# One block in place of two: the prologue of a two-layer transformer kernel is merged into its first projections

## The chip, the cores and the metric

The program runs on one core of a Trainium2 chip. Its time is the time of one execution on the device, in microseconds (us); lower is better. The core has five engines with a queue of instructions each: TensorE (PE in the rows, its weight loads PEld), VectorE (DVE), ScalarE (ACT), GpSimd (POOL) and SyncE (SP), which here only starts transfers. Queues run in order, and engines wait for each other through semaphores.

## The reference, cut to what matters

```python
D_MODEL, SEQ, CTX_LEN = 1024, 1024, 256
mod = jax.nn.silu(c) @ ada_w[l] + ada_b[l]            # 6 x 1024 values, of c and of c_ctx
sh1, sc1, g1, sh2, sc2, g2 = split(mod, 6)
hc = modulate(rms_norm(ctx, norm1_g[l]), csh1, csc1)  # 256 tokens
hx = modulate(rms_norm(x, norm1_g[l]), sh1, sc1)      # 1024 tokens
cb, cc, cx, r, k, v, w_lo, a_lo, g_lo = split_proj(h @ lp["w_in"])
...                                                   # scan, output, feed-forward, second layer
def rms_norm(x, g): return x * rsqrt(mean(x * x, -1) + eps) * g
def modulate(h, shift, scale): return h * (1 + scale) + shift
```

The change touches only this beginning: the modulation of the first norm, the norm itself, and the order of the first products with `w_in`. The scan, the feed-forward part and the second layer stay as they are.

## The kernel before, in words

The 1280 tokens (256 of the context, 1024 of the sequence) stand in columns, the 1024 features in 8 tiles of 128 partitions. They are worked in three column groups g: 0 is the context (256 columns), 1 and 2 are the halves of the sequence (512 columns each). All data is float32.

`prologue` is a block of its own. TensorE forms the modulation for shift and scale in 8 groups of weights (`ada`, 1 MB each, three slots): 16 matmuls of 128x128 weights with the two columns of `silu_c`, in `L173`. Between them, after groups 1, 3 and 5, it adds the squares of a column group over the features: 8 matmuls with a matrix of ones (`sums`, L165). ScalarE makes the squares (L188) and the square root (L193); VectorE the reciprocal and the product with the inputs (L206, L208), then, when the modulation is there, `full` (L227): 8 instructions that scale and shift one feature tile each. A high half `h_hi` is rounded from it by ScalarE in one copy of a column group (L197), and the low half `h_lo` is the difference, three feature tiles of it by GpSimd (L243) and five by VectorE (L236). At the end of the block all engines meet and the semaphores are cleared.

`projections` is the next block. A product (`dense`) of one weight tile with one column group is a chunk: 8 feature tiles times 3 matmuls (high by high, high by low, low by high), 24 matmuls in L106. Chunks rotate over 4 PSUM banks. A weight tile is loaded to `raw_in` by SP (L336), rounded by ScalarE (`hi`, L543) and its low half taken by GpSimd (`lo`, L701); one `raw_in` serves all tiles, so the next load waits for `lo`. The first five chunks are `w` of the groups 0, 1, 2 and then `g` of 1, 2; then come `v`, `k`, `r`, and `cc`, `v` of pair 1, `cx` and so on.

Beside them runs the rest of the modulation, 32 rows of `ada_rows` (512 KB each, four slots). ScalarE's queue starts their loads between its other work (`load_mod`, L607), and VectorE multiplies and adds each (`modulation`, L756, L759). VectorE's queue has 18 of them ahead of the keys of group 0, 4 more ahead of the keys of group 1, 4 ahead of group 2, 6 behind, and then `normed`, `products_rk` and `biases`, for which ScalarE's `tanhs` waits, and behind that ScalarE's `hi` of `cx` and GpSimd's `lo` of it.

Of the kernel before, what the change touches and what calls it, by code (L numbers as in the profile page):

```python
# [21 lines left out]
P = 128  # L22
D = 1024
# [88 lines left out]
def prologue(nc, d, t):  # L112


    groups = [(0, CTX, 1), (CTX, BANK, 0), (CTX + BANK, BANK, 0)]
# [4 lines left out]
    with ExitStack() as st:  # L120
        sem = Sems(nc, st, "a_")
        sb = lambda n, s, dt=F32: st.enter_context(nc.sbuf_tensor("a_" + n, s, dt))
        xin = sb("xin", [P, KD, TOK])
        tmp = sb("tmp", [P, KD, TOK])
        rstd = sb("rstd", [P, TOK])
        adaw = sb("adaw", [P, SLOTS_ADA, NADA, KD, P])
        silu_c = t["silu_c"]
        gain = sb("gain", [P, 2, KD])
        ps = [st.enter_context(nc.psum_tensor(f"a_ps{n}", [P, BANK], F32)) for n in range(4)]
        modps = ps[3][:, 0:32].rearrange("p (n c) -> p n c", c=2)  # L130
        vec, con = t["vec"], t["con"]
        block = st.enter_context(nc.Block())

        @block.sync
        def _(sp):
            sp.dma_start(vec, d["vecs"]).then_inc(sem("vecs"), 16)
            sp.dma_start(con, d["consts"]).then_inc(sem("consts"), 16)
            sp.dma_start(xin[:, :, 0:CTX], d["ctxT"]).then_inc(sem("x0"), 16)

            sp.dma_start(t["c_row"], d["c_in"].broadcast_to([P, D])).then_inc(sem("c_row"), 16)  # L140

            def load_ada(i):
                if i >= SLOTS_ADA:
# [12 lines left out]
        @block.tensor
        def _(pe):
            pe.wait_ge(sem("consts"), 16)
            pe.wait_ge(sem("silu_c"), 1)

            def sums(g):
                at, n, _ = groups[g]
                pe.wait_ge(sem("squares"), g + 1)
# [2777 lines left out]
```

## Time and profile before

| | us |
|---|---|
| median of 3 runs | 2723.29 |
| lowest, highest | 2720.49, 2728.4 |
| the profiled execution, its own time | 2734.07 |
| its span (first to last instruction) | 2732.3 |

Busy shares of the span: TensorE 85%, VectorE 53%, ScalarE 30%, GpSimd 21%. The profile gives the granted clock of TensorE as a mean of 0.917 of full speed. A share over the whole span tells little about the first 210 us, which the change touches; the rows below are of this stretch.

### The profile page before, as it was taken

How to read it: one execution, taken by the hardware profiler on the slowest of the kernel's cores; microseconds unless marked ns; L12 is line 12 of the kernel's file. 1: busy time of each engine (PE TensorE's matmuls, PEld its weight loads, DVE VectorE, ACT ScalarE, POOL GpSimd, SP SyncE). 2: the span in 40 equal slices, each digit the busy share in tenths (PEclk: the TensorE clock that was granted, in tenths of full speed). 3: DMA queues.
4: the chain of work that ended last, by engine and by line, in shares of the span. 5: the costliest groups of instructions: out<-in, count | busy, mean ns of one | idle time of the engine just before them, and what ended most of it. 6: DMA issues, size and time to landing. Idle time of an engine off the chain costs nothing. (4 is left out here: it accounts for less than half of the span.)

```text
span 2732.3 us, 45148 instructions
## 1 busy us (share of the span) xinstructions
PE 2311.8 (85%) x18624; PEld 1864.0 (68%) x18624; DVE 1459.6 (53%) x1855; ACT 812.5 (30%) x1228; POOL 575.7 (21%) x241
## 2 busy tenths in 40 slices
PE   8598987935899969679999996888949999999898
PEld 6476665634889937568788885667738767766566
DVE  1575675748767353446666665111073566644653
ACT  2223333311333331423333332222233344423321
POOL 0313333310000023122222221324232211111111
PEclk8699999976999979889999998999969999999999
DMA  6172342365666451011222223333121111111411
GB/s 233 72 249 74 94 137 73 95 193 128 157 156 153 110 220 47 16 39 69 73 73 74 75 74 119 134 121 129 36 73 59 70 45 49 47 55 39 170 69 70
DMA packets 258244, 271.09 MB, mean 99 GB/s; under 512 B 173080, under 2 KB 208536, under 8 KB 250784
## 3 DMA queue, kind: packets, MB, share of 16 engines
q1 hardware_dynamic: 253472, 251.94, 28.6%
q10 hardware_dynamic: 4608, 16.78, 1.7%
q8 instruction: 126, 2.06, 0.3%
q14 instruction: 38, 0.31, 0.0%
HBM read 200.48 MB, written 68.19 MB: 98 GB/s over the span
## 5 line engine op out<-in xcount | busy, mean ns | idle before, releaser
L106 PE MATMUL e_ps<-h_hi,e_w_hi 128*128 128x512 f32 x704 | 276.1, 392 | 33.1 <-POOL e_w_lo L1942 33.1
L1966 DVE SCALAR_TENSOR_TENSOR e_acc<-e_grid,vec,e_acc 128x1024 f32<-128x1024 f32 x176 | 264.3, 1502 | 42.8 <-DVE e_acc L1966 37.4
L106 PE MATMUL e_ps<-h_hi,e_w_lo 128*128 128x512 f32 x704 | 274.8, 390 | 0.0
L106 PE MATMUL e_ps<-h_lo,e_w_hi 128*128 128x512 f32 x704 | 274.8, 390 | 0.0
L106 PE MATMUL b_ps<-h_hi,b_w_hi 128*128 128x512 f32 (+1 forms) x488 | 196.0, 402 | 72.2 <-POOL b_w_lo L701 42.9
L1942 POOL TENSOR_TENSOR e_w_lo<-raw_up,e_w_hi 128x1024 fp32r<-128x1024 f32 x44 | 116.2, 2642 | 372.2 <-ACT e_w_hi L1913 372.2
L106 PE MATMUL g_ps<-h_hi,g_w_hi 128*128 128x512 f32 x392 | 160.6, 410 | 40.1 <-POOL g_w_lo L2580 35.2
L2580 POOL TENSOR_TENSOR g_w_lo<-raw,g_w_hi 128x1024 fp32r<-128x1024 f32 x38 | 92.9, 2445 | 472.9 <-ACT g_w_hi L2451 472.9
L106 PE MATMUL b_ps<-h_lo,b_w_hi 128*128 128x512 f32 (+1 forms) x488 | 189.5, 388 | 0.0
L106 PE MATMUL b_ps<-h_hi,b_w_lo 128*128 128x512 f32 (+1 forms) x488 | 189.4, 388 | 0.0
L2070 PE MATMUL f_ps<-f_z_hi,f_w_hi 128*128 128x512 f32 x352 | 141.3, 401 | 49.6 <-DVE f_z_lo L2118 39.8
L106 PEld LDWEIGHTS e_ps<-h_hi,e_w_hi 128*128 128x128 f32 x704 | 132.7, 188 | 66.1 <-issue 38.9
L106 PEld LDWEIGHTS b_ps<-h_hi,b_w_hi 128*128 128x128 f32 x488 | 97.9, 201 | 106.2 <-issue 46.2
L106 PE MATMUL g_ps<-h_lo,g_w_hi 128*128 128x512 f32 x392 | 154.8, 395 | 0.0
L106 PE MATMUL g_ps<-h_hi,g_w_lo 128*128 128x512 f32 x392 | 154.5, 394 | 0.0
L106 PEld LDWEIGHTS e_ps<-h_hi,e_w_lo 128*128 128x128 f32 x704 | 132.6, 188 | 27.9
L106 PEld LDWEIGHTS e_ps<-h_lo,e_w_hi 128*128 128x128 f32 x704 | 132.8, 189 | 26.9
L2070 PE MATMUL f_ps<-f_z_lo,f_w_hi 128*128 128x512 f32 x352 | 139.6, 397 | 0.0
L2070 PE MATMUL f_ps<-f_z_hi,f_w_lo 128*128 128x512 f32 x352 | 139.5, 396 | 0.0
L2024 POOL TENSOR_TENSOR f_w_lo<-raw_down,f_w_hi 128x2816 fp32r<-128x2816 f32 x15 | 93.6, 6242 | 196.3 <-ACT f_w_hi L2052 196.3
L2108 DVE SCALAR_TENSOR_TENSOR x<-f_ps,mod,x 128x512 f32 (+1 forms) x16 | 12.0, 751 | 203.4 <-PE f_ps L2070 203.4
L2070 PEld LDWEIGHTS f_ps<-f_z_hi,f_w_hi 128*128 128x128 f32 x352 | 67.7, 192 | 68.5 <-issue 35.8
(338 smaller groups left out, 5147.0 us busy)
## 6 DMA issues: line engine op xcount, KB each, us to landing
raw_up<-w_ffn SPq DMA_DIRECT2D x22, 1024.0 KB, 5.0
raw_down<-w_down SPq DMA_DIRECT2D x16, 1408.0 KB, 6.1
c_op<-ops SPq DMA_DIRECT2D x40, 512.0 KB, 4.4
raw<-w SPq DMA_DIRECT2D x38, 512.0 KB, 3.5
b_ops<-ada_rows ACTq DMA_DIRECT2D x32, 512.0 KB, 5.2
ops<-b_ops SPq DMA_DIRECT2D x16, 1024.0 KB, 4.9
raw_in<-w SPq DMA_DIRECT2D x26, 512.0 KB, 4.6
zs<-e_z SPq DMA_DIRECT2D x22, 512.0 KB, 2.6
```

The lines of the kernel that those rows point to most:

```text
L106: last = nc.tensor.matmul(out, w[:, k, :], x[:, k, cols], start=(k == 0 and n == 0), stop=(k == nk - 1 and n == 2))
L1942: nc.gpsimd.tensor_tensor(w_lo[:, s], raw[:, s], w_hi[:, s].bitcast(F32), ALU.subtract).then_inc(sem(f"lo{s}"), 1)
L1966: a = nc.vector.scalar_tensor_tensor(out=acc[:], in0=view, scalar=wt, in1=acc[:], op0=ALU.mult, op1=ALU.add)
L2024: nc.gpsimd.tensor_tensor(w_lo[:, s], raw[:, s], w_hi[:, s].bitcast(F32), ALU.subtract).then_inc(sem(f"lo{s}"), 1)
L2070: mm = nc.tensor.matmul(ps[s][:], w[:, s, k], y[:, k], start=(k == 0 and n == 0), stop=(k == NFF - 1 and n == 2))
L2108: nc.vector.scalar_tensor_tensor(out=xs, in0=ps[s][:].unsqueeze(1), scalar=t["mod"][:, 0, bass.ds(held(nc.vector, tile + 40), 1)], in1=xs, ...
L2580: nc.gpsimd.tensor_tensor(w_lo[:, w % 2], raw[:, w % 2], w_hi[:, w % 2].bitcast(F32), ALU.subtract).then_inc(sem("lo"), 1)
```

## The change

Both functions become one block, `projections`. In it:

- the loads are issued in another order: first group of `ada` second, the constants behind the context;
- VectorE adds the 8 tiles of squares up to 2 in two instructions (`folded`), and TensorE's `sums` has 2 matmuls in place of 8;
- `h_hi` is written by ScalarE straight from the normed inputs, feature tile by feature tile, with gain and shift in the instruction (`inputs_hi`, 8 instructions for a column group). `full` remains on VectorE and feeds only `h_lo`. The low half of group 0 is VectorE's alone;
- the end of the prologue's block with its clearing of semaphores is gone;
- the first chunks are `w` 0, `w` 1, `g` 1, `w` 2, `g` 2, and each `w` waits for its own column group only;
- the slots of the 32 row loads, and the later tensors, share memory with the inputs, so the first row load waits for the last low half; 16, 20 and 24 rows stand ahead of the keys of the three groups where 18, 22 and 26 stood.

```diff
-def prologue(nc, d, t):
...
-                for k in range(KD):
-                    mm = nc.tensor.matmul(ps[g][:, 0:n], t["c_ones"], tmp[:, k, at:at + n],
-                                          start=(k == 0), stop=(k == KD - 1))
...
+            def sums(g):
+                pe.wait_ge(sem("folded"), 2 * g + 2)
+                for kt in range(2):
+                    mm = nc.tensor.matmul(ps[g][:, 0:width(g)], t["c_ones"], tmp[:, kt, cols(g)], start=kt == 0, stop=kt == 1)
...
             def dense(x, n, g):
+                if n == 0 and x == "w":
+                    pe.wait_ge(sem("h_lo"), g + 1)
+                    if g:
+                        pe.wait_ge(sem("h_lo_pool"), g)
...
             def load_mod(i):
-                if i >= MOD_SLOTS:
+                if i < MOD_SLOTS:
+                    act.wait_ge(sem("h_lo"), 3)
+                    act.wait_ge(sem("h_lo_pool"), 2)
...
+            def inputs_hi(g):
+                act.wait_ge(sem("gain"), 1)
+                act.wait_ge(sem("normed"), g + 1)
+                for kt in range(KD):
+                    a = A(h_hi[:, kt, cols(g)], tmp[:, kt, cols(g)], ACT.Identity, scale=gain[:, c, kt:kt + 1],
+                          bias=t["mod"][:, c, kt:kt + 1])
...
+            hi("w", 0); inputs_hi(0); hi("g", 0); inputs_hi(1); inputs_hi(2); hi("v", 0)
...
+            lo("w", 0); lo("g", 0); inputs_lo(1); inputs_lo(2)              # GpSimd
...
+            full(0); inputs_lo(0); full(1); inputs_lo(1); full(2); inputs_lo(2)   # VectorE
...
-            for g, i in ((0, 18), (1, 22), (2, 26)):
+            for g, i in ((0, 16), (1, 20), (2, 24)):
```

TensorE's queue at the start of the program. Before (`a_adaw` is the slot of a group of `ada`, `con` the matrix of ones):

```order
L173 MATMUL a_ps<-silu_c,a_adaw 128x2 [waits a_ada0,a_silu_c,a_consts]
L173 MATMUL a_ps<-silu_c,a_adaw 128x2 x15
L173 MATMUL a_ps<-silu_c,a_adaw 128x2 [waits a_ada1]
L173 MATMUL a_ps<-silu_c,a_adaw 128x2 x15
L165 MATMUL a_ps<-a_tmp,con 128x256 [waits a_squares]
L165 MATMUL a_ps<-a_tmp,con 128x256 x7
```

And of the change (`b_ada_in` is the slot now, `b_folded` the semaphore of VectorE's folding):

```order
L315 MATMUL b_ps<-silu_c,b_ada_in 128x2 [waits b_ada_in0,b_silu_c]
L315 MATMUL b_ps<-silu_c,b_ada_in 128x2 x15
L315 MATMUL b_ps<-silu_c,b_ada_in 128x2 [waits b_ada_in1]
L315 MATMUL b_ps<-silu_c,b_ada_in 128x2 x15
L306 MATMUL b_ps<-b_tmp,con 128x256 [waits b_folded,b_consts]
L306 MATMUL b_ps<-b_tmp,con 128x256
```

Six matmuls of each `sums` are gone, the first matmul waits for the constants no more, and the first `sums` waits for VectorE.

VectorE's queue from the modulation on. Before:

```order
L218 SCALAR_TENSOR_TENSOR a_gain<-mod,vec 128x8
L227 TENSOR_SCALAR a_tmp<-a_tmp,a_gain,mod 128x256 [waits a_normed,a_gain]
L227 TENSOR_SCALAR a_tmp<-a_tmp,a_gain,mod 128x256 x7
L227 TENSOR_SCALAR a_tmp<-a_tmp,a_gain,mod 128x512 x8
L236 TENSOR_TENSOR h_lo<-a_tmp,h_hi 128x5x256 [waits a_hi]
L227 TENSOR_SCALAR a_tmp<-a_tmp,a_gain,mod 128x512 x8
L236 TENSOR_TENSOR h_lo<-a_tmp,h_hi 128x5x512 [waits a_hi] x2
```

And of the change:

```order
L832 SCALAR_TENSOR_TENSOR b_gain<-mod,vec 128x8
L840 TENSOR_SCALAR b_xin<-b_tmp,b_gain,mod 128x256 [waits b_normed,b_gain]
L840 TENSOR_SCALAR b_xin<-b_tmp,b_gain,mod 128x256 x7
L847 TENSOR_TENSOR h_lo<-b_xin,h_hi 128x8x256 [waits b_full,b_h_hi]
L840 TENSOR_SCALAR b_xin<-b_tmp,b_gain,mod 128x512 x8
L847 TENSOR_TENSOR h_lo<-b_xin,h_hi 128x5x512 [waits b_full,b_h_hi]
L840 TENSOR_SCALAR b_xin<-b_tmp,b_gain,mod 128x512 x8
L847 TENSOR_TENSOR h_lo<-b_xin,h_hi 128x5x512 [waits b_full,b_h_hi]
```

The low half of group 0 now stands directly behind `full` of group 0 and covers all eight feature tiles.

ScalarE's queue around the first products, of the change (`b_wpool` holds the rounded weights, `b_chunk` counts finished chunks, `b_xin` is the memory of the row slots; L561 and L562 read `w`, L564 reads `g`):

```order
L461 ACTIVATE b_wpool<-raw_in 128x1024 [waits b_ada_used2,b_raw]
L536 ACTIVATE h_hi<-b_tmp,mod,b_gain 128x256 [waits b_normed,b_gain]
L536 ACTIVATE h_hi<-b_tmp,mod,b_gain 128x256 x7
L461 ACTIVATE b_wpool<-raw_in 128x1024 [waits b_ada_used0,b_raw]
L536 ACTIVATE h_hi<-b_tmp,mod,b_gain 128x512 [waits b_normed,b_gain]
L536 ACTIVATE h_hi<-b_tmp,mod,b_gain 128x512 x7
...
L562 ACTIVATE b_tmp<-b_ps 64x512
L528 DMA b_xin<-ada_rows 128x1024 [waits b_h_lo_pool,b_h_lo] x4
```

The first weight tile is rounded ahead of the inputs, and the first four row loads, which stood at the head of the second block, now stand behind the reading of `w` of group 1 and wait for the last low halves.

## Rows read from the trace of the kernel before

**Rows 1.** Timeline of TensorE, 0 to 120 us: start, us, engine, line, operation, count.
```profile
13.38 13.79 PE L173 MATMUL a_ps<-silu_c,a_adaw 128*128 128x2 f32 x64 [13.38 <-DMA a_adaw<-ada]
27.03 6.28 PE L165 MATMUL a_ps<-a_tmp,con 128*128 128x256 f32 x16
33.14 11.35 PE L173 MATMUL a_ps<-silu_c,a_adaw 128*128 128x2 f32 x64
44.35 9.58 PE L165 MATMUL a_ps<-a_tmp,con 128*128 128x512 f32 x16
53.76 11.48 PE L173 MATMUL a_ps<-silu_c,a_adaw 128*128 128x2 f32 x64
65.10 9.44 PE L165 MATMUL a_ps<-a_tmp,con 128*128 128x512 f32 x16
74.38 11.59 PE L173 MATMUL a_ps<-silu_c,a_adaw 128*128 128x2 f32 x64
```
**Rows 2.** Timeline of TensorE's weight loads in the second `sums`.
```profile
47.05 0.34 PEld L165 LDWEIGHTS a_ps<-a_tmp,con 128*128 128x128 f32 x1 [0.52 <-issue]
47.90 0.34 PEld L165 LDWEIGHTS a_ps<-a_tmp,con 128*128 128x128 f32 x1 [0.52 <-issue]
```
**Rows 3.** Windows of TensorE: busy (records), granted clock, DMA share, GB/s.
```profile
32.40:36.00 3.60, 3.60 (x30) 0.95 0.01 5
36.00:44.00 8.00, 8.00 (x39) 0.50 0.38 131
119.20:124.20 5.00, 4.93 (x23) 0.50 0.59 226
160.80:164.80 4.00, 3.93 (x11) 0.50 0.77 238
```
**Rows 4.** Timeline of ScalarE, inputs as they arrive, and the transfer of one group of `ada` (issues: count, KB each, us to landing).
```profile
10.67 1.06 ACT L185 ACTIVATE c_row<-c_row 128x1024 f32<-128x1024 f32 x1 [7.17 <-DMA c_row<-c_in]
28.43 3.62 ACT L188 ACTIVATE a_tmp<-a_xin 128x4096 f32<-128x4096 f32 x1 [4.00 <-DMA a_xin<-xT]
...
a_adaw<-ada SPq DMA_DIRECT2D x8, 1024.0 KB, 8.1
```
**Rows 5.** Timelines of VectorE and GpSimd, from the modulation to the products.
```profile
86.01 0.26 DVE L213 TENSOR_TENSOR mod<-a_ps,vec 128x16 f32<-128x16 f32 x2 [2.90 <-PE a_ps L173]
94.22 8.39 DVE L227 TENSOR_SCALAR a_tmp<-a_tmp,a_gain,mod 128x512 f32<-128x512 f32 x8
106.29 2.82 DVE L236 TENSOR_TENSOR h_lo<-a_tmp,h_hi 128x2560 fp32r<-128x2560 f32 x1 [0.95 <-ACT h_hi L197]
...
96.63 3.42 POOL L243 TENSOR_TENSOR h_lo<-a_tmp,h_hi 128x1536 fp32r<-128x1536 f32 x1 [0.66 <-ACT h_hi L197]
106.34 6.05 POOL L243 TENSOR_TENSOR h_lo<-a_tmp,h_hi 128x1536 fp32r<-128x1536 f32 x1 [6.29 <-ACT h_hi L197]
116.88 2.34 POOL L701 TENSOR_TENSOR b_w_lo<-raw_in,b_w_hi 128x1024 fp32r<-128x1024 f32 x1 [4.48 <-ACT b_w_hi L543]
```
**Rows 6.** Timeline of ScalarE's row loads and the first product's start.
```profile
113.58 2.12 ACTq L607 DMA_DIRECT2D b_ops<-ada_rows  x4
...
119.27 0.58 PE L106 MATMUL b_ps<-h_hi,b_w_hi 128*128 128x256 f32 x1 [33.30 <-POOL b_w_lo L701]
```
**Rows 7.** Timeline of TensorE and VectorE, 130 to 210 us, the places where they resume.
```profile
160.87 0.69 PE L451 MATMUL b_ps<-con,b_v 128*128 128x128 f32 x2 [6.10 <-ACT b_v L562]
208.75 0.50 PE L106 MATMUL b_ps<-h_hi,b_w_hi 128*128 128x512 f32 x1 [2.34 <-POOL b_w_lo L701]
...
172.65 0.35 DVE L808 TENSOR_SCALAR b_kk<-b_k,vec 128x256 f32<-128x256 f32 x1 [9.38 <-ACT b_k L562]
202.75 0.16 DVE L764 TENSOR_SCALAR b_bias<-vec 128x4 f32<-128x4 f32 x1
```
**Rows 8.** Waits up to 230 us: total, times, longest.
```profile
ACT b_w_hi L543 <- DMA raw_in<-w: 20.2, 3, 9.3
```
**Rows 9.** Groups of VectorE, 172.5 to 203 us: count, busy, mean ns, idle before.
```profile
L756 DVE CUSTOM_DVE_ANT_0 b_ops<-b_ops,c_row 128x1024 f32<-128x1024 f32 x14 | 19.3, 1377 | 0.2 <-DMA b_ops<-ada_rows 0.2
```

More of the change, by code:

```diff
@@ L420, in dense @@
                         pe.wait_ge(sem("read_d"), dve_read[old])
[L421 removed]
+                product(nc, ps[i % 4][:, 0:width(g)], *weights(s), h_hi, h_lo, KD, cols(g)).then_inc(sem("chunk"), 1)
             def low_rank(m, j):
@@ new lines, in _ @@
+            act.wait_ge(sem("vecs"), 16)
+            A(silu_c, t["v_cc"].rearrange("p (k c) -> p k c", c=2), ACT.Silu).then_inc(sem("silu_c"), 1)
+            act.wait_ge(sem("c_in"), 16)
+            A(c_row, c_row, ACT.Silu).then_inc(sem("c_row"), 1)
+            for g in range(3):
+                act.wait_ge(sem(f"x{g}"), 16)
+                A(tmp[:, :, cols(g)], xin[:, :, cols(g)], ACT.Square).then_inc(sem("squares"), 1)
+            act.wait_ge(sem("eps"), 2)
+            for g in range(3):
+                act.wait_ge(sem("sumsq"), g + 1)
+                A(rstd[:, cols(g)], ps[g][:, 0:width(g)], ACT.Sqrt, scale=1.0 / D, bias=t["c_eps"]).then_inc(sem("std"), 1)
@@ L611, in _ @@
             hi("w", 0)
+            inputs_hi(0)
             hi("g", 0)
[L613 to L623 removed]
@@ new lines, in gains @@
+            def gains():
+                for s in range(SLOTS_ADA):
+                    dve.wait_ge(sem(f"ada_used{s}"), (GADA - 1 - s) // SLOTS_ADA + 1)
+                for c in range(2):
+                    TT(t["mod"][:, c, 0:16], modps[:, :, c], t["v_ada_b"][:, 0:16], ALU.add).then_inc(sem("mod"), 1)
+                dve.wait_ge(sem("mod"), 2)
+                for c in range(2):
+                    a = STT(out=gain[:, c], in0=t["mod"][:, c, 8:16], scalar=1.0, in1=t["v_norm1_g"], op0=ALU.add, op1=ALU.mult)
+                a.then_inc(sem("gain"), 1)
+                dve.wait_ge(sem("gain"), 1)
+                dve.wait_ge(sem("normed"), 3)
@@ new lines, in full, with inputs_lo @@
+            def full(g):
+                c = 1 if g == 0 else 0
+                for kt in range(KD):
+                    a = TS(xin[:, kt, cols(g)], tmp[:, kt, cols(g)], gain[:, c, kt:kt + 1], t["mod"][:, c, kt:kt + 1], ALU.mult, ALU.add)
+                a.then_inc(sem("full"), 1)
+            def inputs_lo(g):
+                k0 = KPOOL if g else 0
+                dve.wait_ge(sem("h_hi"), g + 1)
+                dve.wait_ge(sem("full"), g + 1)
+                TT(h_lo[:, k0:KD, cols(g)], xin[:, k0:KD, cols(g)], h_hi[:, k0:KD, cols(g)].bitcast(F32),
+                   ALU.subtract).then_inc(sem("h_lo"), 1)
@@ L859, in _ @@
+            nc.vector.memset(t["c_eps"], RMS_EPS).then_inc(sem("eps"), 1)
+            nc.vector.memset(t["c_gneps"], GN_EPS).then_inc(sem("eps"), 1)
+            folded(0)
+            inputs_normed(0)
+            folded(1)
+            folded(2)
+            inputs_normed(1)
+            inputs_normed(2)
+            gains()
+            full(0)
+            inputs_lo(0)
+            full(1)
+            inputs_lo(1)
+            full(2)
+            inputs_lo(2)
             TS(ka1[:], k_a, -1.0, 1.0, ALU.mult, ALU.add).then_inc(sem("ka1"), 1)
+            dve.wait_ge(sem("h_hi"), 3)
```

273 lines of the change are left out of this document (112 added, 161 removed).

## The prediction

> **What bounds the kernel now.** The change touches only what lies ahead of about 210 us, so I read three views of that stretch: TensorE's timeline, to see where it works and where it stands; the windows, for its clock; and the timelines of VectorE, ScalarE and GpSimd where TensorE stands.
>
> Up to 86 us TensorE is the bound. It starts at 13.38 and runs without a pause to 85.97 [rows 1], and VectorE waits for its last record [rows 5]. From start to start the four stretches of modulation take 13.65, 11.21, 11.34 and 11.59 us (47.8 for 256 records, two for each matmul) and the three `sums` 6.11, 9.41 and 9.28 us (24.8). The pace of the modulation is 8.00 us for 39 records at granted clock 0.50 (1.2 GHz) and 3.60 us for 30 at 0.95 [rows 3]. The first stretch, 13.65 us for 64 records or 0.213 each, runs at the slow pace. The later stretches save 2.1 to 2.4 us each, because the clock is high for some us behind each run of `sums`. In the second one the weight loads stand 0.85 us apart [rows 2]; 9.41 us for 16 records is 6 at 0.855 and 10 at half of it, so the clock rose 5.1 us into the run.
>
> From 86.0 to 119.27 TensorE stands: 33.3 us for scaling, rounding, the low halves, the end of the block and the first weight tile [rows 5, 6]. Then it works to 154.77, stands 6.1 us for ScalarE's reading of `v`, and works from 160.87 up to a wait of 2.34 us that ends at 208.75 [rows 7]. That last wait is the end of VectorE's queue: keys of group 0 at 172.65, 14 rows of modulation, `normed`, `biases` at 202.75, then 6.0 us through `tanhs`, `hi` and `lo` of `cx`. VectorE has nearly no idle time in it [rows 9], so here two chains are within 2.3 us of each other. Whatever this point (208.75) moves by, I carry to the end: each later step waits for an earlier one of the same block or for its end, and no later instruction is changed.
>
> **The change part by part.** I follow four marks.
>
> *Mark 1, the modulation is there (before 86.0).* The start: the first group of `ada` (1.05 MB [rows 4]) was the fifth transfer and is the second now. By the shapes, the bytes up to its end fall from 3.8 to 1.24 MB, and between the two ScalarE rows that wait for inputs 7.3 MB came in 17.8 us, 0.41 MB/us [rows 4]. Going back from `c_row` (2.76 MB, 10.67) gives 6.8 us: -6.6. The `sums`: 4 records in place of 16. The clock needs a run that the new `sums` don't have: 4 records of 512 columns are 3.4 us at the slow pace of 0.855 and end before it could rise, those of 256 columns 1.7: 8.5 us in all, -16.3. But then the clock stays at 1.2 GHz, and the modulation takes 256 x 0.213 = 54.6 us: +6.8. Lastly TensorE is now ahead of its data: group 1 (4.86 MB) is there at 15.8 where TensorE wants it at 13.7, group 3 (11.7 MB, behind both halves of x and the first weight tile) at 32.2 where it wants it at 31.2: +3.1. Sum: 6.8 + 54.6 + 8.5 + 3.1 = 73.0, or -13.0. The folding (per column group 6 column tiles more on VectorE, at 1.1 ns a column by the 2560 columns in 2.82 us [rows 5]: 1.7 or 3.4 us) lies behind the squares at 32.1 and ahead of the `sums` at 39, so it is hidden. `normed` of group 2 ends at about 68 and is hidden too, with 5 us to spare.
>
> *Mark 2, the first product (before 119.27).* 0.5 us for the gain; 8 high halves of 256 columns by ScalarE, which the trace before doesn't have in this form. ScalarE's passes over 1024 and 4096 columns take 1.06 and 3.62 us [rows 4]: 0.83 ns a column and 0.21 us fixed. Eight of 256 columns cost 8 x 0.42 = 3.4 us, or 1.7 if the fixed parts overlap wholly. I take 3.0, nearer the upper end. Then the low half of 2048 columns, 2.3 us. The first weight tile is ready by then (rounded before the gain, GpSimd's part done at about 64). 73.0 + 5.8 = 78.8, which is -40.5. The clearing and the meeting of the engines (6.05 us of GpSimd's last row end at 112.4, the new block starts at 113.6 [rows 5, 6]) are in this.
>
> *Mark 3, `v` of group 1 done (before 154.77).* `w` 0 takes 5.2 us at the low clock as before, to 84.0. Then TensorE waits for the low half of group 1. ScalarE rounds the tile of `g` (1.06) and is done with `h_hi` 1 (8 x 0.59, the fixed part partly hidden) at about 82.3. `full` 1 starts at 78.8 and takes 3.6 us alone, but GpSimd's `lo` of `g` (2.34 us) falls into it. Next to a GpSimd subtraction of 3.42 us, 8 such instructions took 8.39 us [rows 5]. So it ends between 82.4 and 85; I take 83.7. GpSimd's three tiles then take 6.05 us as in the row beside VectorE's own subtraction, to 89.7. TensorE stands 5.7 us. After that come the same chunks as before, 30.4 us from 124.4 to 154.77, and `w` 2 isn't late: its low half is there at 100 to 101, and TensorE wants it at 102. The wait of 5.7 us lets the clock fall: after the stand of 6.1 us TensorE had 0.50 for 4 us [rows 3, 7], which costs 2.0 us. 89.7 + 30.4 + 2.0 = 122.1: -32.7. So 7.8 us of what mark 2 gained are given back here.
>
> The Trainium skill ("SBUF — State Buffer", section "SBUF: two separate sides") calls the read and write ports that VectorE and GpSimd share an exclusive lock, held for a whole instruction, with the loser fully blocked. The row of 8.39 us beside one of 3.42 agrees. By that rule alone `full` 1 would end at 84.7, and mark 3 would be 1.0 us later.
>
> *Mark 4, `cx` starts (before 208.75).* The stand at `v` was ScalarE's wait for the weight tile `r`, whose load waits for `g` 2 to be read. That now happens at about 114.5, and the load lands 4 to 9 us later (the longest of such waits was 9.3 us [rows 8]), so ScalarE reads `v` between 120 and 125; TensorE resumes at 123.5 (-37.4). The stand shrinks from 6.1 to 1.4 us. TensorE would then be at `cx` 45.5 us later, 169.0. VectorE: row loads start at 100.5 and not at 113.58, only 13 us earlier [rows 6], since they wait for the last low half. 16 rows must be done at the keys of group 0, which stand 11.8 us behind TensorE's start [rows 7], at 135.3. Four slots, 5 us each plus 1.4 on VectorE, and ScalarE's queue between them: worked row by row that comes to 134. It is a tie. After the keys there are 16 rows and not 14, at 1.38 us [rows 9]: 135.3 + 30.1 + 2.8 is `biases` at 168.2 and `cx` at 174.2, if VectorE keeps its pace; if it is quicker, TensorE's own 169.0 is the bound. I take 172.3, nearer the pace that the rows show: -36.5.
>
> **Sum.** 2734.07 - 36.5 = 2697.6 for an execution like the profiled one, which is 10.8 above the median of 2723.29. The median should go to 2686.8. A change of less than 0.3%, 8 us, can't be told from none.
>
> **The rivals.**
>
> - *The row loads set the pace.* For: they start only 13 us earlier. Before, 18 rows took from 113.58 to about 163.3, 2.76 us each, with VectorE idle for much of it. At that pace 16 take 44 us, to 144.7, and `cx` starts at 144.7 + 32.9 + 6 = 183.6: -25. That gives 2698. Against: much of that idle time was ScalarE's queue waiting for products and for the tile `r`, which come earlier too.
> - *The clock stays or rises.* If the three short `sums` raise the clock after all, the 6.8 us come back and so does part of the 3.1: up to -44, 2679. The row in which it rose only 5 us into a run speaks against it.
> - *Slower than before.* The first products are now broken by stands. If the clock fell in each and stayed at 1.2 GHz, a chunk of 512 columns would take 24 x 0.43 = 10.3 us, not 5.44: 4.9 us each. From the eighth such chunk on the gain of 36.5 is gone, and with 11 it is 2723.3 + 17 = 2741. Against it: the clock rose 5 us after the start at 119.2 and 4 us after 160.8 [rows 3], each time in the first chunk.
> - *Nothing changes.* This needs a later wait that ends at a fixed time whatever comes before. I see none: the scan starts when the block has ended.
>
> **How the numbers follow.** Forecast 0.60; row loads 0.15; a faster start (clock, less blocking) 0.19; slower 0.03; nothing 0.03. The bounds of the unknown terms are: high halves 1.7 to 3.4, `full` 1 by 2.6, arrival of `r` 5, VectorE's pace 5.2, clock 2 and 6.8. Not all fall the same way, so the range runs from -49 to -22: 2674 to 2701, which takes in both rivals. Faster 0.95, same 0.02, slower 0.03.
>
> **What would show it.** (1) Start of TensorE's modulation at 6 to 8 us; clock 0.50 up to 73 and 31 to 32 matmul records (16 matmuls) of a group in 6.8 us; short waits for `ada` at about 14 and 31. (2) 5 to 6.5 us from the modulation to the first product. (3) A stand of 4 to 8 us behind `w` 0, which GpSimd's low half ends. (4) First row load at 99 to 102. (5) `cx` of pair 0 at about 172. The prediction is wrong if the modulation is there before 68 or after 78, if the row loads keep VectorE idle behind the first keys, or if the time beyond `cx` isn't that of before.

## The result and the profile after

| | before | changed |
|---|---|---|
| median of 4 runs each, us | 2721.89 | 2692.11 |
| lowest, highest | 2715.26, 2728.4 | 2689.1, 2696.83 |
| ratio of the medians, 95% | | 0.9892 (0.9864 to 0.9921) |
| the profiled execution, its span | 2732.3 | 2687.3 |

The change makes the kernel 29.8 us faster (by the interval 21.5 to 37.0). The forecast was a gain of 36.5 us and a median of 2687 us, with a range from 2674 to 2701.

The page of the changed kernel, its section of busy times, changes little. TensorE is busy for 21.2 us less (2311.8 before), and of the 45.0 us by which the span is shorter the rest is time in which it stood.

```profile
span 2687.3 us, 45063 instructions
PE 2290.6 (85%) x18588; PEld 1853.5 (69%) x18588; DVE 1472.8 (55%) x1861; ACT 818.7 (30%) x1249; POOL 567.7 (21%) x240
```

Timeline of TensorE in the changed kernel, from 0 to the second chunk (start, us, engine, line, operation, count, idle before and what ended it). It answers to [rows 1, 6].

```profile
6.73 6.96 PE L315 MATMUL b_ps<-silu_c,b_ada_in 128*128 128x2 f32 x32 [6.73 <-DMA b_ada_in<-ada]
15.66 6.99 PE L315 MATMUL b_ps<-silu_c,b_ada_in 128*128 128x2 f32 x32 [1.97 <-DMA b_ada_in<-ada]
22.51 2.05 PE L306 MATMUL b_ps<-b_tmp,con 128*128 128x256 f32 x4
24.35 6.83 PE L315 MATMUL b_ps<-silu_c,b_ada_in 128*128 128x2 f32 x32
33.02 6.99 PE L315 MATMUL b_ps<-silu_c,b_ada_in 128*128 128x2 f32 x32 [1.84 <-DMA b_ada_in<-ada]
41.41 3.78 PE L306 MATMUL b_ps<-b_tmp,con 128*128 128x512 f32 x4 [1.40 <-DVE b_tmp L816]
44.98 10.55 PE L315 MATMUL b_ps<-silu_c,b_ada_in 128*128 128x2 f32 x64
55.39 3.76 PE L306 MATMUL b_ps<-b_tmp,con 128*128 128x512 f32 x4
58.94 10.55 PE L315 MATMUL b_ps<-silu_c,b_ada_in 128*128 128x2 f32 x64
76.57 0.58 PE L106 MATMUL b_ps<-h_hi,b_wpool 128*128 128x256 f32 x1 [7.08 <-DVE h_lo L847]
...
88.56 0.76 PE L106 MATMUL b_ps<-h_hi,b_wpool 128*128 128x512 f32 x1 [7.48 <-issue]
```

The reader sees the early start, three short waits, and the last two stretches of 64 records in 10.55 us. At the pace of the first groups (6.83 for 32) they would take 13.65. The first product starts at 76.57 and not at 119.27.

Timelines of VectorE, GpSimd and ScalarE in the changed kernel, from the modulation to the row loads (L847 and L663 are low halves of the inputs, L840 is `full`, L643 is `lo` of a weight tile, L528 starts a row load). They answer to [rows 5, 6].

```profile
69.59 0.26 DVE L829 TENSOR_TENSOR mod<-b_ps,vec 128x16 f32<-128x16 f32 x2 [1.87 <-PE b_ps L315]
...
74.23 2.29 DVE L847 TENSOR_TENSOR h_lo<-b_xin,h_hi 128x2048 fp32r<-128x2048 f32 x1 [1.40 <-ACT h_hi L536]
76.44 5.79 DVE L840 TENSOR_SCALAR b_xin<-b_tmp,b_gain,mod 128x512 f32<-128x512 f32 x8
82.34 2.83 DVE L847 TENSOR_TENSOR h_lo<-b_xin,h_hi 128x2560 fp32r<-128x2560 f32 x1
85.08 6.86 DVE L840 TENSOR_SCALAR b_xin<-b_tmp,b_gain,mod 128x512 f32<-128x512 f32 x8
...
75.22 3.54 POOL L643 TENSOR_TENSOR b_wpool<-raw_in,b_wpool 128x1024 fp32r<-128x1024 f32 x1 [11.97 <-ACT b_wpool L461]
82.38 6.08 POOL L663 TENSOR_TENSOR h_lo<-b_xin,h_hi 128x1536 fp32r<-128x1536 f32 x1 [3.63 <-DVE b_xin L840]
...
70.16 4.04 ACT L536 ACTIVATE h_hi<-b_tmp,mod,b_gain 128x256 fp32r<-128x256 f32 x8 [9.34 <-DVE b_gain L832]
74.10 1.04 ACT L461 ACTIVATE b_wpool<-raw_in 128x1024 fp32r<-128x1024 f32 x1
75.05 11.39 ACT L536 ACTIVATE h_hi<-b_tmp,mod,b_gain 128x512 fp32r<-128x512 f32 x16
...
98.31 2.50 ACTq L528 DMA_DIRECT2D b_xin<-ada_rows  x3
```

GpSimd's low half of group 1 ends at 88.46, and the stand of 7.48 us in TensorE's row ends 0.1 us later. The row says "issue" where it waited for two semaphores, but this is the one that came last. The first row load starts at 98.31.

Timelines in the changed kernel, 119 to 176 us: of TensorE every row with idle time before it, of VectorE the keys of group 0 (134.53) and `biases` (168.22), and behind them the rows of ScalarE and GpSimd that lead to `cx` [rows 7]:

```profile
123.26 0.44 PE L367 MATMUL b_ps<-con,b_tmp 128*128 128x128 f32 x2 [2.04 <-ACT b_tmp L480]
170.74 0.45 PE L346 MATMUL b_ps<-b_tmp,b_xin 64*128 64x256 f32 x1 [3.09 <-ACT b_xin L509]
174.21 0.79 PE L106 MATMUL b_ps<-h_hi,b_wpool 128*128 128x512 f32 x1 [2.77 <-POOL b_wpool L643]
...
134.53 0.35 DVE L760 TENSOR_SCALAR b_tmp<-b_tmp,vec 128x256 f32<-128x256 f32 x1 [1.57 <-ACT b_tmp L480]
168.22 0.16 DVE L716 TENSOR_SCALAR b_bias<-vec 128x4 f32<-128x4 f32 x1
...
168.46 1.28 ACT L509 ACT_TABLE_LOAD   x1 [8.61 <-DVE b_bias L716]
...
171.62 2.54 POOL L643 TENSOR_TENSOR b_wpool<-raw_in,b_wpool 128x1024 fp32r<-128x1024 f32 x1 [0.32 <-ACT b_wpool L461]
```

`biases` is at 168.22 and `cx` at 174.21, 34.5 us earlier than before. TensorE stands twice there (3.09 and 2.77 us), both times behind VectorE's queue by way of ScalarE and GpSimd. So VectorE's rows from the keys of group 0 on set this point. At the keys themselves VectorE waits 1.57 us for ScalarE's copy of TensorE's product, so up to there the chain runs through TensorE.

In the following the scan is the stretch from its own first matmul to the first matmul of the block behind it. The 45.0 us between the two profiled spans are 34.5 us up to `cx` (208.75 to 174.21), 5.7 from `cx` to the scan's first matmul (374.1 and 368.5 us long), 2.7 in the scan (397.1 and 394.4) and 2.1 behind it (1752.3 and 1750.2). The scan's start is read from the views of its PSUM tile, here of the kernel before and of the changed one:

```profile
L1078 PE MATMUL c_ps<-c_pre x640: 218/218/366, 582.9 to 801.9; 64*64 64x64 f32 x160
```
```profile
L1084 PE MATMUL c_ps<-c_pre x640: 217/219/367, 542.7 to 762.7; 64*64 64x64 f32 x160
```

### The profile page after: what moved, and what is told of

It is laid out like the page before. It is cut to its first block and busy times, and to the rows that moved or that the text cites. A ratio compares the mean times of both kernels' runs of the same rounds, so it can differ in the third digit from the quotient of the medians.

```text
span 2687.3 us, 45063 instructions
## 1 busy us (share of the span) xinstructions
PE 2290.6 (85%) x18588; PEld 1853.5 (69%) x18588; DVE 1472.8 (55%) x1861; ACT 818.7 (30%) x1249; POOL 567.7 (21%) x240
## 5 line engine op out<-in xcount | busy, mean ns | idle before, releaser
L106 PE MATMUL b_ps<-h_hi,b_wpool 128*128 128x512 f32 (+1 forms) x976 | 310.1, 395 | 52.0 <-DVE b_tmp L785 25.5
L106 PEld LDWEIGHTS b_ps<-h_hi,b_wpool 128*128 128x128 f32 x976 | 189.4, 200 | 102.8 <-issue 53.1
L106 PE MATMUL b_ps<-h_lo,b_wpool 128*128 128x512 f32 (+1 forms) x488 | 189.3, 388 | 0.0
L1948 POOL TENSOR_TENSOR e_w_lo<-raw_up,e_w_hi 128x1024 fp32r<-128x1024 f32 x44 | 107.3, 2439 | 381.3 <-ACT e_w_hi L1919 381.3
L106 PEld LDWEIGHTS g_ps<-h_hi,g_w_hi 128*128 128x128 f32 x392 | 74.7, 190 | 56.6 <-POOL g_w_lo L2586 36.2
```

The lines of the kernel that those rows point to most:

```text
L106: last = nc.tensor.matmul(out, w[:, k, :], x[:, k, cols], start=(k == 0 and n == 0), stop=(k == nk - 1 and n == 2))
L1948: nc.gpsimd.tensor_tensor(w_lo[:, s], raw[:, s], w_hi[:, s].bitcast(F32), ALU.subtract).then_inc(sem(f"lo{s}"), 1)
```

## The experiments

After the result there were four open questions: why the clock gave more than forecast, why the time measured less than the profiles, what each part of the change is worth, and whether a better version exists. All marks are of one profiled execution each, in us. M is the moment when VectorE takes the modulation (69.59 above), and `w` 1 is the first product with column group 1 (88.56 above).

| kernel | M | M to first product | M to `w` 1 | M to `cx` | `cx` at | `cx` to scan | scan |
|---|---|---|---|---|---|---|---|
| before | 86.01 | 33.3 | | 122.7 | 208.8 | 374.1 | 397.1 |
| before2 | 85.96 | 33.2 | | 121.8 | 207.8 | 369.3 | 396.9 |
| changed | 69.59 | 7.0 | 19.0 | 104.6 | 174.2 | 368.5 | 394.4 |
| rep | 75.88 | 7.0 | 19.0 | 107.0 | 182.9 | 368.5 | 401.6 |
| no_fold | 80.59 | 7.0 | 18.9 | 104.6 | 185.2 | 369.8 | 400.5 |
| all_wait | 69.41 | 28.6 | | 119.5 | 188.9 | 369.5 | 395.1 |
| old_hi | 69.46 | 9.1 | 20.7 | 105.0 | 174.5 | 368.1 | 398.8 |
| pair | 71.56 | 7.0 | 19.0 | 106.7 | 178.3 | 369.9 | 393.0 |
| kpool0 | 69.60 | 7.0 | 17.2 | 103.6 | 173.2 | 369.1 | 394.9 |
| best | 69.28 | 7.0 | 15.2 | 99.2 | 168.5 | 370.5 | 395.3 |
| old_dma | 77.45 | 7.0 | 19.0 | 105.2 | 182.7 | 369.6 | 394.2 |
| old_order | 75.81 | 7.0 | 19.0 | 110.0 | 185.8 | 368.5 | 394.6 |
| rows18 | 75.90 | 7.0 | 19.0 | 106.2 | 182.1 | 370.0 | 396.1 |
| best18 | 65.69 | 7.3 | 15.5 | 100.4 | 166.1 | 370.2 | 398.0 |

Two columns answer a question of their own. From `cx` to the scan every kernel but the first takes 368.1 to 370.5, so what is gained at `cx` arrives at the scan. The scan itself takes 393.0 to 401.6 in code that no kernel here changes: this 8.6 us is the spread of single executions, and a gain of a few us is read from the marks rather than from a span.

**rep**: the changed kernel as it is, timed six times more.

> The changed kernel itself, unchanged, in more rounds. In the two profiles the first product of cx starts 34.5 us earlier than before and the last instruction 45 us earlier; the medians differ by 29.8 us. Theory A: the change is worth what it moves the start of cx, 34 to 39 us with what the three loops over the pairs add; the rest of the 45 is spread from execution to execution. Then the median lies 30 to 40 us below before (ratio 0.985 to 0.989), and marks up to cx repeat within 1 us while later ones spread by several. Theory B: later parts gain or lose by the change itself; then the stretch behind cx is again about 10 us shorter than in the profile of before.

Measured: 2699.81, ratio 0.9906 (0.9876 to 0.9936). M came at 75.88, 6.3 us later than in the first profile of the same kernel. Timeline of TensorE in rep, the last rows ahead of M:

```profile
41.49 3.78 PE L306 MATMUL b_ps<-b_tmp,con 128*128 128x512 f32 x4 [1.56 <-DVE b_tmp L816]
45.07 13.65 PE L315 MATMUL b_ps<-silu_c,b_ada_in 128*128 128x2 f32 x64
58.59 3.76 PE L306 MATMUL b_ps<-b_tmp,con 128*128 128x512 f32 x4
62.14 13.65 PE L315 MATMUL b_ps<-silu_c,b_ada_in 128*128 128x2 f32 x64
```

Up to 45 us the two executions agree within 0.15 us. Then the 64 records take 13.65 and not 10.55, twice. The first pace is that of granted clock 0.50 in [rows 3], 1.2 GHz; in the other execution the clock rose to 2.4 GHz behind the `sums` for a part of the stretch. Of the eight profiles with `sums` of 3.6 us four have the one (changed, all_wait, old_hi, kpool0) and four the other (rep, old_dma, old_order, rows18). So this part of the change is worth 16.4 us in one execution and 10.1 in another. Windows of TensorE in the changed kernel (busy, records, granted clock, DMA share, GB/s) show the mean clock of the two stretches:

```profile
45.00:55.50 10.50, 10.50 (x66) 0.69 0.28 100
59.00:69.50 10.50, 10.49 (x65) 0.66 0.16 50
```

The timed executions without a trace can be sorted too, since the span and the mean granted clock of each are on record. Of the eight profiled ones the four that took 10.55 us have a mean of 0.925 to 0.928, and the four that took 13.65 have 0.931 to 0.934. (The slower ones have the higher mean because the record keeps 1.00 in them up to about 90 us, as the last section shows.) By this mark the clock stayed low in 18 of the 40 timed executions of the kernels with short `sums`: in 1 of 4 of the changed kernel at first, and in 4 of 6 here. Over its ten executions the median is 2692.6 us with the clock raised and 2700.5 without, five executions each. The mark is an inference from means and doesn't carry over to kernels with longer `sums`: the fastest execution of `best` below, 2678.16 us, has 0.931 as well.

**no_fold**: only the folding is undone.

```diff
-                pe.wait_ge(sem("folded"), 2 * g + 2)
-                for kt in range(2):
+                pe.wait_ge(sem("squares"), g + 1)
+                for kt in range(KD):
```

> The folding on VectorE is undone: TensorE adds all 8 tiles of squares again (8 matmuls for a column group). Theory A (TensorE is the bound up to the modulation): the three sums cost 24.8 us and not 9.0, of which some 4 us hide in waits for data that TensorE then doesn't have; the modulation is there at about 81 us where it is at 69.6 now, and the whole 11 to 12 us reach the end (ratio to before 0.992 to 0.994). Theory B (the row loads or VectorE's chain set the later pace): less than 6 us reach the end.

Measured: 2701.53, ratio 0.9921 (0.989 to 0.9951). M is 11.0 us later than in the changed profile and 4.7 later than in rep. Timeline of TensorE in no_fold:

```profile
48.52 11.21 PE L315 MATMUL b_ps<-silu_c,b_ada_in 128*128 128x2 f32 x64
59.59 9.71 PE L306 MATMUL b_ps<-b_tmp,con 128*128 128x512 f32 x16
69.14 11.35 PE L315 MATMUL b_ps<-silu_c,b_ada_in 128*128 128x2 f32 x64
```

The long `sums` raise the clock in each profile that has them (this one, before and before2), and the modulation behind them takes 11.2 to 11.6. Start to start, no_fold spends 24.7 us in `sums` (rep: 9.0), 45.7 in its 256 records (rep: 54.8, changed: 48.6) and 2.6 in waits for data (5.3, 5.2), and it began 0.8 later. So the folding removes 15.7 us, and gives back 9.1 or 2.9 by the clock and 2.7 by waits. `cx` is 11.0 us later than in the changed profile and 2.4 later than in rep. The medians of rep and no_fold, 1.7 us apart on one chip, don't resolve what is left. None of the six executions of no_fold has a mean clock of 0.931 or more; its median of 2701.5 lies near the 2700.5 of the changed kernel's low clock and 9 us above its 2692.6. Most of what the folding is worth thus hangs on whether the clock rises.

**all_wait**: the first products wait for the low halves of all three column groups.

```diff
-                    pe.wait_ge(sem("h_lo"), g + 1)
-                    if g:
-                        pe.wait_ge(sem("h_lo_pool"), g)
+                    pe.wait_ge(sem("h_lo"), 3)
+                    pe.wait_ge(sem("h_lo_pool"), 2)
```

> The first products wait for the low halves of all three column groups, as the block's end made them do before; all else is that of the change. Theory A: the first product starts at about 98.3 and not at 76.6; v of group 1 is done at about 134 and not at 121.2, since the 7.5 us stand and one slow start of the clock go; 10 to 12 us of it reach the start of cx and the end. Theory B (the rows of modulation, whose loads don't move here, are the bound behind the first products): 5 us or less reach cx.

Measured: 2705.87, ratio 0.9939 (0.9915 to 0.9964). TensorE stands 28.71 us ahead of its first product:

```profile
98.02 0.55 PE L106 MATMUL b_ps<-h_hi,b_wpool 128*128 128x256 f32 x1 [28.71 <-issue]
```

M to `cx` grows by 14.9 us. The row loads moved too, which I had not expected: they stand in ScalarE's queue behind the reading of `w` of group 1, so they start at 109.16 and not at 98.31, and of the 14.9 us 12.7 are there when `v` of group 1 is done (133.7 and 121.2), the rest comes behind it. Of the 18.1 us that the change gains from M to `cx`, the products by column group are thus by far the largest part. The 3.2 us that are left (2.3 against before2) hold everything else behind M, the end of the old block with its clearing of semaphores among it, and no run takes them apart.

**old_hi**: ScalarE rounds `h_hi` from `full` in one copy of a column group again.

```diff
-                act.wait_ge(sem("gain"), 1)
-                act.wait_ge(sem("normed"), g + 1)
...
+                act.wait_ge(sem("full"), g + 1)
+                A(h_hi[:, :, cols(g)], xin[:, :, cols(g)], ACT.Copy).then_inc(sem("h_hi"), 1)
```

> The high halves are rounded again in one copy for a column group from the scaled inputs, with VectorE's order of before (full 0, full 1, low half 0, full 2, low halves 1 and 2). Theory A: the direct form is worth next to nothing, since 8 instructions of 0.51 us (256 columns) take 4.0 us against 2.7 of full plus 1.9 of one copy: the first product comes 0.5 to 2.5 us later, the products of group 1 start within 2 us of 88.6, the end moves by -1 to +3 us. Theory B: rounding from the normed inputs is a main part of the gain, and the end is 5 us or more later.

Measured: 2696.42, ratio 0.9907 (0.9876 to 0.9938). Counted from M, the first product is 2.2 us later, `w` 1 1.8, and at `cx` 0.4 us are left. Writing the high halves straight from the normed inputs is worth next to nothing here, since VectorE's rows set `cx` and the first row load even starts a little earlier (27.9 us behind M, not 28.7).

**before2**: the kernel before, one more execution, to see how well a profile of it repeats.

> The kernel before itself, for a second profile. Theory: up to the end of the prologue it repeats, because its runs of sums are long enough to raise TensorE's clock each time: modulation there at 86 us within 2, start of cx at 208.8 within 3. The changed kernel's two profiles differ by 6.3 us there. If before varies by 5 us or more too, the forecast's term of the clock is not what sets the two profiles of the change apart.

Measured: its own time 2723.91, span 2722.1, ten below the first one. M is the same to 0.05 us. Of the 10.2 us the first profile had 1.0 more ahead of `cx`, 4.8 between `cx` and the scan, 0.2 in the scan and 4.2 behind it. The profile on which the forecast rests was thus a long one, mostly behind `cx`, and the forecast's allowance for it (its own time is 10.8 above the median) was right.

**pair**: the `sums` of groups 1 and 2 stand together behind the fifth group of `ada`.

```diff
+                    if i == 1:
...
+                        sums(0)
+                    if i == 4:
+                        sums(1)
+                        sums(2)
```

> The changed kernel with the sums of groups 1 and 2 one behind the other, after group 4 of the modulation weights. In its profiles so far the clock rose in two of the short sums of the one execution (modulation there at 69.6 us) and in none of the other (75.9). Theory A: a run of 3.6 us raises the clock by chance, one of 7.1 us does each time: the last 96 records of the modulation are quicker by 2 to 3 us than at the slow pace, TensorE waits for no folding, and the modulation is there at 70 to 72.5. Theory B: the clock stays at 0.50 in such a run too, and the modulation is there at 74 to 76.

Measured: 2692.14, ratio 0.9899 (0.9867 to 0.9931). Timeline of TensorE in pair:

```profile
47.18 6.50 PE L306 MATMUL b_ps<-b_tmp,con 128*128 128x512 f32 x8
53.52 17.95 PE L315 MATMUL b_ps<-silu_c,b_ada_in 128*128 128x2 f32 x96
```

96 records at the slow pace take 20.48 us (best has such a row), so the clock was up for a part of this stretch, but there is only one such stretch and not two. M is at 71.56: between the two profiles of the changed kernel. The run of 8 records raised the clock in all three profiles that have it (pair 6.50 us, best 6.41, best18 5.19). All its four executions have a mean clock of 0.925 to 0.928, and its median is near the 2692.6 of the changed kernel's executions with the clock raised. But M to `cx` is 2.1 us longer than in the changed profile.

**kpool0**: GpSimd has no part in the inputs' low halves; VectorE takes all eight feature tiles.

```diff
-    KPOOL = 3
+    KPOOL = 0
```

> The changed kernel with all low halves of the inputs taken by VectorE, none by GpSimd. Theory A (the two exclude each other, so the shared work takes the sum of both: GpSimd's 6.1 us beside VectorE's 2.8): VectorE alone takes 4.5 us for a group of 512 columns, the products of group 1 start 1.7 us earlier against the modulation (17.3 us behind it and not 19.0), full of group 2 takes 3.7 us and not 6.9, and the first row load starts 2 to 3 us earlier (26 and not 28.7 us behind). Theory B (they work side by side): the products of group 1 start later, as VectorE has more to do and GpSimd's share saved time.

Measured: 2692.84, ratio 0.9904 (0.9871 to 0.9936). `w` 1 starts 1.7 us earlier, the row loads 1.3, `cx` 1.0. Timelines of VectorE and GpSimd in kpool0:

```profile
76.45 5.80 DVE L835 TENSOR_SCALAR b_xin<-b_tmp,b_gain,mod 128x512 f32<-128x512 f32 x8
82.35 4.43 DVE L842 TENSOR_TENSOR h_lo<-b_xin,h_hi 128x4096 fp32r<-128x4096 f32 x1
86.69 5.80 DVE L835 TENSOR_SCALAR b_xin<-b_tmp,b_gain,mod 128x512 f32<-128x512 f32 x8
...
75.23 3.53 POOL L640 TENSOR_TENSOR b_wpool<-raw_in,b_wpool 128x1024 fp32r<-128x1024 f32 x1 [12.10 <-ACT b_wpool L459]
87.48 2.44 POOL L640 TENSOR_TENSOR b_wpool<-raw_in,b_wpool 128x1024 fp32r<-128x1024 f32 x1 [8.71 <-ACT b_wpool L459]
```

`full` 2 (at 86.69) was expected to fall from 6.86 us to 3.7 and fell only to 5.80: GpSimd's `lo` of the next weight tile, which had waited behind its part of the inputs, now fell into it. One GpSimd instruction was taken away and another took its place.

**best**: kpool0 and pair; the tile of `g` is rounded ahead of the inputs' high halves; all foldings ahead of the first norm and the fourth group of `ada` ahead of the last inputs.

```diff
             hi("w", 0)
-            inputs_hi(0)
             hi("g", 0)
+            inputs_hi(0)
...
             folded(0)
-            inputs_normed(0)
             folded(1)
             folded(2)
+            inputs_normed(0)
```

> Four edits together: no GpSimd in the low halves; the weight tile of g rounded ahead of the high halves of the inputs, so that GpSimd's work on it doesn't fall into full of group 1; the folding of all groups ahead of the first norm and the fourth group of modulation weights ahead of the last inputs; the sums of groups 1 and 2 together. By the rows of the change: products of group 1 at 15.1 us behind the modulation (19.0 now), first row load at 24 (28.7), modulation there at 68 to 71 us, cx at 166 to 171 us (174.2 and 182.9 in the two profiles). If the row loads set VectorE's pace, cx moves as they do, by 4 to 5 us against the modulation; if TensorE does, by 3 to 4. The median is 8 to 12 us below that of the change (ratio to before 0.984 to 0.988). The rival: the gain ends in the wait at the tile r, and nothing is faster by more than 3 us.

Measured: 2682.29 (2678.16 to 2683.51), ratio 0.9857 (0.9833 to 0.9881), the lowest of all; pair and kpool0, timed beside it on the same chip, lie 10 us above. Their intervals overlap its own a little, but each of its six executions is below each of their eight (highest 2683.51, lowest 2688.48). What each of the other edits in it is worth was not taken apart. Timelines of VectorE, GpSimd and TensorE in best:

```profile
76.13 3.74 DVE L839 TENSOR_SCALAR b_xin<-b_tmp,b_gain,mod 128x512 f32<-128x512 f32 x8
79.97 4.42 DVE L846 TENSOR_TENSOR h_lo<-b_xin,h_hi 128x4096 fp32r<-128x4096 f32 x1
...
64.05 3.12 POOL L644 TENSOR_TENSOR b_wpool<-raw_in,b_wpool 128x1024 fp32r<-128x1024 f32 x1 [4.60 <-ACT b_wpool L463]
...
123.10 0.63 PE L369 MATMUL b_ps<-con,b_tmp 128*128 128x128 f32 x4 [0.98 <-ACT b_tmp L496]
```

GpSimd's `lo` of `g` is over at 67.2, ahead of the modulation, and `full` 1 takes 3.74 us and not 5.8. `w` 1 starts 15.2 us behind M (changed: 19.0), TensorE no longer stands ahead of its first matmuls on `v` (2.04 us in the changed kernel) and only for 0.98 us one step later, and `cx` comes 99.2 us behind M (104.6).

**old_dma**: the constants, the context and `c_in` are loaded ahead of the first group of `ada` again.

```diff
-            load_ada(0)
+            sp.dma_start(con, d["consts"]).then_inc(sem("consts"), 16)
             sp.dma_start(xin[:, :, 0:CTX], d["ctxT"]).then_inc(sem("x0"), 16)
             sp.dma_start(c_row, d["c_in"].broadcast_to([P, D])).then_inc(sem("c_in"), 16)
-            sp.dma_start(con, d["consts"]).then_inc(sem("consts"), 16)
+            load_ada(0)
```

> The first loads in the order of before: constants, context and c ahead of the first group of modulation weights; all else is that of the change. Theory A (TensorE, from its first matmul on, sets when the modulation is there): it starts at 13.4 us and not at 6.7, waits for no second group, and the first sums start 4.6 us later; the modulation is there 3.5 to 5 us later than in the change (69.5 where the clock rises in the short sums, so 73 to 74.5), and cx starts as much later. Theory B: the waits for data behind it eat the early start, and the modulation is there within 1.5 us of 69.5.

Measured: 2694.99, ratio 0.9885 (0.986 to 0.9909). TensorE starts at 14.07 and not at 6.7, but M is at 77.45, only 1.6 us behind rep, rows18 and old_order, the profiles of the same clock. Timeline of TensorE in old_dma, its first rows:

```profile
14.07 13.79 PE L315 MATMUL b_ps<-silu_c,b_ada_in 128*128 128x2 f32 x64 [14.07 <-DMA b_ada_in<-ada]
27.72 2.05 PE L306 MATMUL b_ps<-b_tmp,con 128*128 128x256 f32 x4
29.57 13.65 PE L315 MATMUL b_ps<-silu_c,b_ada_in 128*128 128x2 f32 x64
```

The three waits of 2.12, 1.65 and 1.56 us in rep are gone here. An early start buys only what the next transfers allow: of 7.4 us, 5.3 went into these waits. This was nearer to the smaller of the expected figures. And of the 1.6 us nothing is seen further on: `cx` is at 182.7 here, at 182.9 in rep and at 182.1 in rows18, and the median of 2694.99 is below the 2699.99 and 2700.44 of rows18 and old_order, timed beside it.

**old_order**: the first chunks are `w` 0, 1, 2 and then `g` 1, 2 again.

```diff
-    CHUNKS = [("w", 0, 0), ("w", 0, 1), ("g", 0, 1), ("w", 0, 2), ("g", 0, 2)] + [(x, 0, g) for x, g in V0_FIRST]
+    CHUNKS = [("w", 0, 0), ("w", 0, 1), ("w", 0, 2), ("g", 0, 1), ("g", 0, 2)] + [(x, 0, g) for x, g in V0_FIRST]
```

> The first five products in the order of before: w of the groups 0, 1, 2 and then g. Theory A: w of group 2 is wanted at 96 us and its low half is there at 98.3, so TensorE stands 2.3 us more and v of group 1 is done 2 to 4 us later; against the modulation cx starts 106.5 to 108.5 us behind (104.6 in the change). Theory B: the stand at the tile r, 2.0 us in the change, takes it up and cx moves by less than 1 us.

Measured: 2700.44, ratio 0.9904 (0.988 to 0.9927). `w` 2 now waits 2.54 us for its low half, at 104.49, and M to `cx` is 3.0 us longer than in rep, which has the same clock ahead of M. In time this isn't resolved: the median is within 0.5 us of that of rows18, which has the new order.

**rows18**: 18, 22 and 26 rows of modulation ahead of the keys again.

```diff
-            for g, i in ((0, 16), (1, 20), (2, 24)):
+            for g, i in ((0, 18), (1, 22), (2, 26)):
```

> VectorE has 18, 22 and 26 rows ahead of the keys of the three groups as before, and not 16, 20 and 24. Theory A (the forecast's term: 16 rows behind the keys of group 0 in place of 14 cost 2.8 us): cx starts 2 to 3 us earlier, 102 us behind the modulation. Theory B: VectorE has the same 32 rows in either order and waited only 1.6 us at these keys, so that is all that two more rows there can fill: cx moves by 0 to 1.6 us.

Measured: 2699.99, ratio 0.9891 (0.986 to 0.9922). M to `cx` is 106.2, against 107.0 in rep. The 0.8 us are less than the 2.4 by which the two profiles of the changed kernel differ there, and best18 below moves the other way: no gain from the number of rows ahead of the keys is shown, and all 32 rows are worked before `cx` either way.

**best18**: best with 18, 22 and 26 rows.

> The four edits of the faster version and 18, 22 and 26 rows ahead of the keys. In the faster version VectorE waits 0.64 us at the keys of group 0. By theory B of the run on rows alone nothing is to be had: cx at 168.5 us within 1 and the ratio to before within 0.001 of 0.986. By theory A cx starts 2 to 3 us earlier, at 166.

Measured: 2685.52 (2684.25 to 2688.57), ratio 0.9858 (0.9839 to 0.9877), so best repeats against a second baseline, 2724.51, and the rows again bring nothing (M to `cx` 100.4 and 99.2). Its M of 65.69 is the earliest of all: the run of two `sums` took 5.19 us and not 6.4, and the 96 records behind it 16.06 us.

## Why the prediction was right, point by point

The sign was right, and so were the four places where the time is won or given back; the gain was forecast 6.7 us too high, inside its range. That it came so near is in part luck. The forecast counts with a clock that stays low ahead of M. The profile in which it does so is rep: `cx` comes there at 182.9 and not at 172.3, 10.6 us later than forecast, and the median of that measurement is only 22.8 us below the kernel before, at the lower edge of the range. A clock that rose, by its mean (see rep), in three of the first four timed executions, which the forecast had left to a rival, made up for 7.0 of the 13.7 us that this median lacks to the forecast. Each mark is compared by the distance to the one before, since a mark inherits the error of the earlier ones.

**Mark 1, forecast 73.0, measured 69.59 and 75.88 (rep).** The terms of 6.8 (start), 54.6 (256 records), 8.5 (`sums`) and 3.1 (waits) measured 6.7, 54.8, 9.0 and 5.3 in rep. The term that is off most there is the waits, by 2.2: two for data were foreseen, the third, 1.56 us for VectorE's folding ahead of the `sums` of group 1, was called hidden and isn't. It stands in VectorE's queue behind the reciprocal and the product of group 0 (33.81 to 37.8 in the changed profile), which the forecast didn't count, and so it ends at 41.4 and not ahead of 39. (Two figures of the forecast are slightly off by its own rate of 0.41 MB/us: the start is 7.0 and not 6.8, the arrival of group 3 32.5 and not 32.2.) In the changed profile the records took 48.6 us and not 54.6. The step that failed is that the short runs "end before it could rise": the clock can rise, in four of the eight profiles and by the mean clock in 22 of 40 timed executions, and the forecast should have carried both, 69.6 and 75.9, in place of a rival of 0.19. That the single row in which it rose 5.1 us into a run excludes a rise in one of 3.4 was the false inference.

**Mark 2, forecast 5.8 behind the modulation, measured 7.0.** (7.3 in best18; 28.6 in all_wait and 9.1 in old_hi, whose edits lie here.) The term of eight high halves was mis-sized: 4.04 us, and not 3.0. A pass of 256 columns costs 0.51 us and one of 512 0.71, where the fit through long copies gave 0.42 and 0.63. The sum lies outside the 5 to 6.5 us that the forecast had named as its sign for this step.

**Mark 3, forecast 43.3 behind mark 2 (10.9 to `w` 1, then 32.4), measured 44.6 (12.0 and 32.6).** GpSimd's low half took 6.08 us (6.05 forecast) and ended the stand, as said. `full` 1 took 5.79 us and not 4.9. The Trainium skill ("SBUF — State Buffer", section "SBUF: two separate sides") would have given 5.9: by its rule, the loser of the shared ports waits for the whole instruction. The rows agree with it: `full` of 512 columns takes 3.74 us with no GpSimd work beside it (best), 5.80 beside a `lo` of 2.44 (kpool0) and 6.86 beside a low half of 6.08 (above), of which the last 3.3 us lie behind VectorE's own subtraction. The plainest row is a small instruction of VectorE (timeline of VectorE in the changed kernel). It takes 0.16 us in kpool0 and in best; here it lasts until GpSimd's low half of group 2 ends, at 98.2:

```profile
94.78 3.47 DVE L865 TENSOR_SCALAR b_ka<-vec 128x4 f32<-128x4 f32 x1
```

The forecast read the 8.39 us of [rows 5] as the effect of one GpSimd instruction of 3.42. There were two: one of 4.70, from 91.28 on, ran into the first 1.8 us of this `full` as well.

**Mark 4, forecast 50.2 behind mark 3, measured 53.0 (rep: 55.9).** The stand at `v` is 2.04 us (1.4 forecast). The tie between the two chains was decided for VectorE: `cx` came at 174.21, the upper of the two bounds, 174.2, and the two stands ahead of it are both VectorE's. The compromise of 172.3 was the failed step; where two chains tie, the later one is the time. But two errors cancel in that number. VectorE's chain had been counted from a mark 1 that was 3.4 us later than in this profile. From M it had 101.2 us to `cx`, and 104.6 were measured: 3.2 of the difference are there when TensorE resumes on `v` (53.7 behind M, 50.5 forecast), as the sum of what marks 2 and 3 and the stand at `v` had too little.

**What lies behind `cx`** was carried unchanged, rightly: 368.5 us to the scan in the changed kernel and in rep, 369.3 in before2.

**The sum.** From M to `cx` the forecast had 99.3 and the changed profile 104.6, 5.3 us more (rep 107.0; of the 2.4 more in rep 1.0 is there when TensorE resumes on `v`, after a stand of 3.49 us, and 2.0 at the keys of group 0, and the cause stays open), and M itself lies 3.4 below or 2.9 above. Against before2 (scan at 577.1) the changed kernel's scan starts 34.4 us earlier and rep's 25.7 us. The timed gains, 29.8 and 22.8 us, lie near these two. By the mean clock the first holds one execution of four with the clock low and the second four of six, which fits the 7.7 us between the medians; with so few executions it isn't shown that the clock is all of this difference.

**The rivals.** Row loads did not set the pace: VectorE waits for rows only well ahead of the keys of group 0 (2.75 us at most behind the first), is done with its 16 rows at 133.0, and the 1.57 us at 134.53 are a wait for the keys. Behind them it waits for rows for 1.4 us in all. The clock did rise, in some executions. It did not stay low in the products: `w` 1 to `v` 1 took 32.6 and 32.1 us with 32.4 forecast.

## What to carry to other kernels

Let an engine start on the first part of its input where it waited for all: of the 18 us between the modulation and `cx`, that gave nearly 15, while fewer passes over the inputs gave 0.4. Count the early start of an engine only as far as its next transfers follow: 7.4 us earlier were 1.6 at the modulation and none at `cx`. Where GpSimd and VectorE work side by side, move GpSimd's instruction to where VectorE is idle, and look which one falls into the gap then; and where two chains tie in a sum, take the later.

## What the hardware showed that was not expected

- Whether TensorE's clock rose in the short `sums` (4 records of 512 columns, 3.6 us) differed between executions of one program, the changed kernel, with 6.2 us between them in two stretches of 64 records. Over all kernels with these `sums` it rose in four profiles and not in four others. A run of 8 such records (5.2 to 6.5 us) raised it in three of three, one of 16 (9.4 us and more) in six of six, and one of 16 records of 256 columns (5.6 to 6.3 us) in three of three (before, before2 and no_fold).
- The granted clock in the profile doesn't fit the pace at the start of a program. Windows of TensorE in rep (busy, records, granted clock, DMA share, GB/s) have 1.00 where the pace is that of 0.50 in [rows 3], some 0.21 us a record:

```profile
45.00:58.50 13.50, 13.50 (x65) 1.00 0.23 78
62.20:75.80 13.60, 13.59 (x65) 1.00 0.11 39
```

- A scan that no kernel here changes varied between 393.0 and 401.6 us in 14 profiles, while what lies behind it stayed within 1747.3 and 1752.3.
